# Gate and up projections as 2x2 blocks with seven block products instead of eight

## The reference, cut to what matters

```python
def _swiglu(x, w_in, w_out):
    gate, up = jnp.split(x @ w_in, 2, axis=-1)
    return (jax.nn.silu(gate) * up) @ w_out
...
h = h + 0.5 * _swiglu(_rms_norm(h, g_ffn), w_ffn_in, w_ffn_out)   # D_MODEL = 1024, D_FF = 2816
```

## Time and profile before

| | us |
|---|---|
| median of 3 runs | 2584.19 |
| lowest and highest | 2573.76, 2585.38 |
| the profiled execution | 2584.06 |
| its span, first to last instruction | 2582.3 |

### The profile page before, as it was taken

The page is one execution under the profiler, slowest core; times in us unless marked ns, Lnnn a source line. Parts: engine busy times, 40 slices in busy tenths (PEclk is TensorE's granted clock), DMA queues, the critical chain, the costliest instruction groups (busy, mean ns, idle before and its releaser), DMA issues.

```text
span 2582.3 us, 46166 instructions
## 1 busy us (share of the span) xinstructions
PE 2454.5 (95%) x18130; PEld 2369.9 (92%) x18130; DVE 1158.5 (45%) x1551; ACT 821.8 (32%) x1370; POOL 316.1 (12%) x331
## 2 busy tenths in 40 slices
PE   7999999599898999999999999999979999999997
PEld 7999999588888999999977999999868889999997
DVE  5433443455654544344444443444455545443443
ACT  4222222444544322122322221223245543221221
POOL 2000000243432100000122000001132211000001
PEclk9999999799998999999999999999988889999999
DMA  3232221000000223222223222222211102232221
GB/s 118 89 113 74 89 95 63 28 10 17 11 23 17 90 83 109 73 89 97 68 81 110 89 89 91 82 91 89 82 32 44 34 26 89 88 101 72 89 97 68
DMA packets 84937, 187.18 MB, mean 72 GB/s; under 512 B 42129, under 2 KB 43697, under 8 KB 84865
## 3 DMA queue, kind: packets, MB, share of 16 engines
q1 hardware_dynamic: 83584, 181.68, 22.4%
q0 software_dynamic: 1280, 4.49, 0.5%
HBM read 178.79 MB, written 7.35 MB: 72 GB/s over the span
## 4 chain that ended last, share of the span: by engine, by line
PE 88%; DVE 5%; ACT 3%; issue 2%; POOL 1%; DMA 0%; ACTq 0%; DVEq 0%; POOLq 0%; SPq 0%
PE ps L493 65%; PE ps L468 6%; PE ps L470 6%; PE ps L469 6%; PE ps L712 3%; PE ps L718 1%; PE ps L665 1%; ACT arena L1016 1%; DVE x_lo L1226 1%; POOL stat L1707 1%; DVE stat L1388 0%; DVE stat L1460 0%; DVE rstd L1231 0%; ACT scratch L1051 0%; DVE x_lo L1224 0%
## 5 line engine op out<-in xcount | busy, mean ns | idle before, releaser
L493 PE MATMUL ps<-x_hi,w_hi 128*128 128x272 f32 x2816 | 586.5, 290 | 18.9 <-DVE w_lo L1214 10.1
L493 PE MATMUL ps<-x_hi,w_lo 128*128 128x272 f32 x2816 | 585.0, 289 | 0.0
L493 PE MATMUL ps<-x_lo,w_hi 128*128 128x272 f32 x2816 | 582.8, 289 | 0.0
L1214 DVE TENSOR_TENSOR w_lo<-raw,w_hi 128x1024 fp32r<-128x1024 f32 (+4 forms) x300 | 397.5, 1327 | 301.7 <-ACT w_hi L875 294.0
L493 PEld LDWEIGHTS ps<-x_hi,w_hi 128*128 128x128 f32 x2816 | 445.4, 189 | 21.3 <-issue 10.1
L875 ACT ACTIVATE w_hi<-raw 128x1024 fp32r<-128x1024 f32 (+4 forms) x300 | 328.8, 1099 | 393.6 <-PE ps L493 250.6
L493 PEld LDWEIGHTS ps<-x_lo,w_hi 128*128 128x128 f32 x2816 | 445.0, 190 | 0.0
L493 PEld LDWEIGHTS ps<-x_hi,w_lo 128*128 128x128 f32 x2816 | 441.8, 190 | 0.0
L493 PE MATMUL ps<-hid_hi,w_hi 128*128 128x272 f32 x1664 | 345.5, 289 | 3.6 <-DVE hid_lo L1224 3.6
L493 PE MATMUL ps<-hid_lo,w_hi 128*128 128x272 f32 x1664 | 344.9, 288 | 0.0
L493 PE MATMUL ps<-hid_hi,w_lo 128*128 128x272 f32 x1664 | 344.5, 288 | 0.0
(11 more groups left out here) (207 smaller groups left out, 3230.7 us busy)
## 6 DMA issues: line engine op xcount, KB each, us to landing
raw<-w_ffn_in SPq DMA_DIRECT2D x176, 512.0 KB, 3.5
raw<-w_ffn_out SPq DMA_DIRECT2D x64, 704.0 KB, 4.0
raw<-w_b_kv SPq DMA_DIRECT2D x16, 512.0 KB, 3.6
raw<-w_a_out SPq DMA_DIRECT2D x8, 512.0 KB, 3.6
raw<-w_b_q SPq DMA_DIRECT2D x8, 512.0 KB, 3.6
raw<-w_b_out SPq DMA_DIRECT2D x8, 512.0 KB, 3.6
raw<-w_a_in SPq DMA_DIRECT2D x4, 672.0 KB, 3.9
raw<-w_a_qup SPq DMA_DIRECT2D x8, 288.0 KB, 2.8
```

The lines of the kernel that those rows point to most:

```text
L493: mm = pe.matmul(pair(bank)[:, n, :], w[a], xs[b][:, cols], start=(k == 0 and a + b == 0), stop=(k == kt - 1 and a == 1))
L1214: dve.tensor_tensor(wl[par][:, 0:n], raw[par][:, 0:n], wh[par][:, 0:n].bitcast(F32), ALU.subtract).then_inc(w_lo, 1)
```

## The change

Gate and up weights of one hidden tile are seen as a 2x2 block matrix (rows: gate, up; columns: the first and the last four of the eight model tiles), and x as a 2x2 block matrix too (rows: model tiles 0 to 3 and 4 to 7; columns: token columns 0 to 271 and 272 to 543). Strassen's method in Winograd's form makes the product with seven block products instead of eight: 7 x 4 x 3 = 84 matmuls of 272 columns for a gate/up pair. For it:

- GpSimd makes four sums of weight blocks for each pair (`weight_sums`, four operations of 128x512), two pairs ahead, and also takes over `hid_lo`.
- The weights of a pair come by two loads (up, then gate) into `R`, twelve blocks of 512 columns, of which two sets of four hold the raw weights and four the sums. ScalarE and VectorE split seven blocks per pair in groups "01", "23", "45" (1024 columns each) and "6" (512).
- x is mixed once per stage: VectorE makes four combinations per pair of model tiles (t1 to t4), ScalarE rounds all seven (816 and 1088 columns) and VectorE takes their low parts into `xs`.
- The results are put together from three PSUM banks (two sets of three, by parity) by ScalarE copies p6, p5 and VectorE's u2, u3, up[1], gate[1] and up[0]. Of the norm only gate is multiplied; the factor for up is applied to the result of the "out" part, in two VectorE operations (`e`, `h`) where there was one.
- The constants for MLA and for the second attention are loaded later, since `R` and `xs` share memory with other tiles.

The core of it, the products on TensorE, the sums on GpSimd, one turn on VectorE and on ScalarE:

```diff
@@ tensor, ffn_in @@
+                def times(par, j, k):
+                    w, b = operand(par, j), 3 * par + (2, 0, 1, 2, 0, 1, 2)[j]
+                    w = [a[:, k * P:(k + 1) * P] for a in w]
+                    return product(ps[:, b, 0:HALF_T], w, [xs_part(n, k, j, j + 1) for n in range(2)],
+                                   j in (0, 1, 2, 3) and k == q["order"][0], k == q["order"][DK - 1], j in (4, 5, 6))
...
+                    for j in range(3, 7):
+                        if j == 3:
+                            pe.wait_ge(*st["act"].at("p6", i))
+                        if j == 4:
+                            pe.wait_ge(*ws.at("45", i))
+                            pe.wait_ge(*st["dve"].at("u2", i))
+                        if j == 5:
+                            pe.wait_ge(*st["act"].at("p5", i))
+                        if j == 6:
+                            pe.wait_ge(*ws.at("6", i))
+                            pe.wait_ge(*st["dve"].at("u3", i))
@@ gpsimd @@
+            def weight_sums(q, m, par, free=()):
...
+                pool.wait_ge(*ws["dve"].at("23", i - 1))
+                pool.wait_ge(up_load[par], loads)
+                pool.tensor_tensor(s1, a21, a22, ALU.add).then_inc(inc, 1)
+                pool.wait_ge(*ws["dve"].at("01", i - 1))
+                pool.wait_ge(gate_load[par], loads)
+                pool.wait_ge(*ws["pool"].at("s1", i))
+                pool.tensor_tensor(s2, s1, a11, ALU.subtract).then_inc(inc, 1)
+                pool.tensor_tensor(s3, a11, a21, ALU.subtract).then_inc(inc, 1)
+                pool.wait_ge(*ws["dve"].at("45", i - 1))
+                pool.wait_ge(*ws["pool"].at("s2", i))
+                pool.tensor_tensor(s4, a12, s2, ALU.subtract).then_inc(inc, 1)
...
+                def turn(m, par, more):
+                    if more:
+                        weight_sums(q, m + 1, par)
+                    i = 2 * m + par
+                    pool.wait_ge(*st["act"].at("hid_hi", i))
+                    pool.tensor_tensor(tile(hid[1], i), scratch[3], tile(hid[0], i).bitcast(F32), ALU.subtract
@@ vector, ffn_in, turn(i) @@
+                    dve.tensor_tensor(u2, bx, p6, ALU.add).then_inc(inc, 1)
...
+                        pair_lo(q, i + 1, 1 - par, "01")
+                    dve.wait_ge(*st["pe"].at("m3", i))
+                    dve.wait_ge(*st["dve"].at("u2", i))
+                    dve.tensor_tensor(u3, by, u2, ALU.add).then_inc(inc, 1)
+                    dve.wait_ge(*st["act"].at("p5", i))
+                    dve.wait_ge(*st["pool"].at("hid_lo", i - 1))
+                    dve.wait_ge(*st["dve"].at("u3", i))
...
+                    dve.tensor_tensor(up[1], u3, p5, ALU.add).then_inc(inc, 1)
...
+                        pair_lo(q, i + 1, 1 - par, "23")
+                    dve.wait_ge(*st["pe"].at("m4", i))
+                    dve.tensor_tensor(gate[0], bx, r[0], ALU.mult).then_inc(inc, 1)
+                    dve.wait_ge(*st["pe"].at("m5", i))
+                    dve.tensor_tensor(gate[1], bz, u2, ALU.add).then_inc(inc, 1)
+                    dve.wait_ge(*st["dve"].at("c12", i))
+                    dve.tensor_tensor(gate[1], gate[1], r[1], ALU.mult).then_inc(inc, 1)
+                    if not last:
+                        pair_lo(q, i + 1, 1 - par, "45")
+                    dve.wait_ge(*st["pe"].at("m6", i))
+                    dve.tensor_tensor(up[0], by, u2, ALU.add).then_inc(inc, 1)
...
+                    dve.tensor_tensor(scratch[3], scratch[0], scratch[3], ALU.mult).then_inc(inc, 1)
+                    if not last:
+                        pair_lo(q, i + 1, 1 - par, "6")
@@ scalar, ffn_in, turn(i): p6, "01", p5, "23", "45", silu, "6", hid_hi @@
+                    act.activation(scratch[2][:, 0:HALF_T], ps[:, y, 0:HALF_T], ACT.Copy).then_inc(inc, 1)
...
+                    act.wait_ge(*st["dve"].at("hid", i))
...
+                    act.activation(tile(hid[0], i), scratch[3], ACT.Copy).then_inc(inc, 1)
@@ sync @@
+            def load_pair(q, i, par):
...
+                sp.wait_ge(*q["ws"]["dve"].at("6", i - (1 if isinstance(i, int) and i == 0 else 2)))
+                src, b = d["w_ffn_in"][q["f"], q["half"], i], a_block(par, 0)
+                for n, done in ((2, up_load[par]), (0, gate_load[par])):
+                    sp.dma_start(R[:, b + n:b + n + 2, :].rearrange("p b w -> p (b w)"),
+                                 src[:, n * HB:(n + 2) * HB]).then_inc(done, 16)
```

More of the change, by code:

```diff
@@ L48 @@
 SLOT = FT * P
+DK = KC // 2
+HB = DK * P
+XW = 7 * HALF_T
 NEG = -1.0e30
@@ L292, in ffn @@
                 kind = "honly" if hf == 0 else "last" if gain is None else "update"
-                parts.append(dict(kind="in", u=units(2 * FT, KC * P), st=run("ffn", FT), f=f, half=hf,
-                                  x=None, rms=None))
-                parts.append(dict(kind="out", what=kind, u=units(KC, FT * P), kt=FT, scale=0.5,
-                                  st=run(kind, KC), src=("ffn", f, hf), gain=gain, first=None))
+                q = dict(kind="in", st=run("pair", FT), ws=run("wsplit", FT), f=f, half=hf, n=HALVES * f + hf,
+                         x=None, rms=None, last_unit=unit[0] - 1, order=list(range(DK)), prev=None, second=None, stores=False)
+                if hf == 1:
+                    q["prev"] = parts[-1]
+                    parts[-1]["next"] = q
+                parts.append(q)
+                parts.append(dict(kind="out", what=kind, u=units(KC, FT * P), kt=FT, st=run(kind, KC),
+                                  src=("ffn", f, hf), gain=gain, first=None, before=q, next=None))
+                q["out"] = parts[-1]
             return parts
-        X0 = run("xsplit", KC)
+        X0 = run("xsplit", DK)
         F0 = ffn(0, G_MIX)
@@ L305, in build @@
                  att=run("att", PAIRS))
-        MO = dict(kind="out", what="update", u=units(KC, KC * P), kt=KC, scale=1.0, st=run("update", KC),
-                  src=("a",), gain=G_FFN + 8, first=M)
+        MO = dict(kind="out", what="supdate", u=units(KC, KC * P), kt=KC, st=run("supdate", DK),
+                  src=("a",), gain=G_FFN + 8, first=M, before=None)
         F1 = ffn(1, G_BKV)
+        MO["next"] = F1[0]
         F1[0].update(x=MO["st"], rms=run("rms"))
@@ L318, in build @@
                  att=run("att", PAIRS), fstage=run("fstage", PAIRS))
-        XO = dict(kind="out", what="update", u=units(KC, KC * P), kt=KC, scale=1.0, st=run("update", KC),
-                  src=("b",), gain=G_FFN + 24, first=X)
+        XO = dict(kind="out", what="supdate", u=units(KC, KC * P), kt=KC, st=run("supdate", DK),
+                  src=("b",), gain=G_FFN + 24, first=X, before=None)
         F3 = ffn(3, None)
+        XO["next"] = F3[0]
         F3[0].update(x=XO["st"], rms=run("rms"))
```

581 lines of the change are left out of this document (422 added, 159 removed).

## The result

The changed kernel takes 2612.13 us, the median of four runs (2609.79 to 2613.2), where the kernel before took 2583.82 in the same comparison. The ratio is 1.0108, with a 95% interval of 1.009 to 1.0126: slower by one per cent where it was forecast one per cent faster, and 55 us above the forecast of 2557. It lies outside the forecast's own range (2538 to 2576) and 0.1 us above the top of the wide one (2480 to 2612). The profiled execution took 2609.79 us, its span 2608.0.

What follows compares the result with a forecast made beforehand. VectorE and GpSimd taking turns at SBUF were to bind the gate/up loop at 11.6 us per tile. Terms -53 + 9 + 13 + 0.4 + 3.2 = -27 us gave 2557 us, own range 2538 to 2576, wide range 2480 to 2612.

Steps and rivals of the forecast that it cites:

- the ring: Gate/up loop: VectorE and GpSimd taking turns at SBUF, with their waits, make 11.6 us per tile against TensorE's 10.52.
- the wait ahead of product 3: Gate/up loop: TensorE waits 1.08 us per tile for p6, which stands on ScalarE behind hid_hi.
- hand-over: Shared SBUF access passing between VectorE and GpSimd: overlap leaves 1.09 of 1.23 us and 1.12 of 1.28 to count.
- Rival 1: Gate/up loop: TensorE stays the bound, 10.52 us a tile, total 2479; chance 0.25 with what lies between.
- rival 2: Gate/up loop: no overlap when VectorE and GpSimd swap access, 12.9 us a tile, total 2640; chance 0.24.
- Rival 3: Gate/up loop: second weight load lands 1.6 us later than counted, 0.8 us a tile, total 2615; chance 0.06.
- A half: Gate/up stage half of 11 pairs: 124.7 us after the change, 7.6 less than 132.3; seven halves save 53.
- rival 4: Gate/up loop: TensorE's idling lowers its clock to 1.2 GHz, costing 1.5 us a tile, mostly hidden; no separate chance.
- The start: First half ends at about 161 us instead of 152.3, after serial rounds on x of some 6.5 us: +9.
- MO, XO: Attention out-projections: late second-unit splits, three waits of 1.1 us, and 3.1 at the end: +6.5 each, 13 together.
- Key/value stage: Passage from key/value stage to layer 1: split "23" (1.23) replaces the first low part (0.8): +0.4 us.
- Way out: Result scaled and added in two operations, uncovered only behind the last tile, four times: +3.2 us.

Runs made afterwards that it cites:

- experiment 1: VectorE's four weight-split subtractions read one operand from cleared PSUM banks, against the changed kernel; 2545.83 us, ratio 0.984 to the kernel before.
- Narrow squares: GpSimd's adding of squares at the start, in MO and in XO on 16 of 544 columns, against the changed kernel; 2590.28 us, ratio 1.0017.
- early split: In MO and XO each second weight unit is split ahead of the rounding and low parts of x, against the changed kernel; 2597.99 us, ratio 1.004.
- late reciprocal: In the first pair of F0, F1 and F3 split "23" goes ahead of the reciprocal, against the changed kernel; 2605.2 us, ratio 1.0081.
- narrow sums: GpSimd's weight sums on 16 of 512 columns from the third pair of each half, against the changed kernel; 2522.16 us, ratio 0.9748.
- experiment 4: Ahead of F2 a key/value store is issued behind GpSimd's sums, against the changed kernel: third store 2614.36 us, fourth store 2612.32 us.

## Why the prediction was wrong

**The loops: right.** 10.52 us of TensorE, 11.6 from the ring (11.70), the wait ahead of product 3 behind p6 (0.86 for 1.08), the lengthened instructions and the counting of 1.09 and 1.12 us for a hand-over all stand. Taking VectorE's second SBUF operand out of four subtractions gave 10.58 without any other change in the loop. Rival 1 (10.52) and rival 2 (12.9) are out; the hand-over does overlap, as far as I counted it. Rival 3's 2615 comes near the measured time by chance: late loads cost almost nothing here (below). The sum of the ring is no full model, though: for another order it gave 11.4 to 11.7, and 12.74 was the common pair in seven of eight halves.

The Trainium skill, "SBUF — State Buffer", section "Who interferes with whom", calls the pair of ports that VectorE and GpSimd share an exclusive lock, and says of VectorE's 2-port modes that whoever issues first has it "for the whole instruction". Worked by the letter for this kernel that was the 12.9 of rival 2, and the trace has 11.70. The section also says that a VectorE instruction contends with GpSimd's reads when both its inputs are in SBUF, and not when at most one is. There trace and page agree: 1950 ns with both in SBUF, 1224 with one in PSUM (experiment 1).

**A half: 6.4 us less, not 7.6.** The second halves gained 5.8 to 6.7. F3's, with no irregular pair, takes 125.7 us: eight pairs of about 11.7 and three of 10.6 to 10.9. So my 0.1 us too little for a bound pair, and 0.04 for a free one, make nearly 4 of the 4.8 us that the four halves lack; F0's is 0.9 longer. Loads landed after 4.5 us in the median, where I took 3.5 from the earlier trace rows. GpSimd's second sum waited for one four times, up to 1.4 us; a short and a long pair follow each time instead of two bound ones. Two such couples by the ends of their last products, in F0 and in F1 (same columns as above):

```profile
271.82:282.41 10.59, 10.59 (x87) 10.59 (x86) 9.56 (x12) 5.49 (x8) 8.09 (x6) 1.00 0.29 99
282.41:296.52 14.11, 12.35 (x87) 12.14 (x86) 12.88 (x14) 5.47 (x8) 10.74 (x8) 0.88 0.22 74
...
1143.56:1154.21 10.65, 10.65 (x87) 10.60 (x86) 9.63 (x12) 5.48 (x8) 7.41 (x6) 1.00 0.31 100
1154.21:1166.80 12.59, 10.83 (x87) 10.61 (x86) 12.43 (x14) 5.48 (x8) 9.30 (x6) 1.00 0.26 83
```

In F1 the two take 23.2, nothing lost. In F0 they take 24.7, since TensorE's clock fell there as well, to 0.50 in the window 290 to 292, after it had idled half of 286 to 288. That is rival 3 and rival 4 in small.

**The start, MO, XO: the step that failed.** I worked out one round on x as a chain of operations with nearly their own durations ("some 6.5 us") and put GpSimd "in between" as if it cost tenths. I had just shown that every two-operand instruction of VectorE may wait 1.1 us for GpSimd, and used it only for the loops. A round has six such instructions, and four of them are the shortest of the kernel. Narrow squares show the size: 22 us in the median, 19 of them in the three profiled stages, and a round of 6.35 us without them. The start came to 20.0 for 9, and the last low part of x ended at 45.2 where I had "about 34"; the waits for every second split were 2.3 for 1.1. The early split took most of them away, 14 us in the median. The 2 us for the reciprocal were too small as well: it holds back "23" and with it GpSimd's sums, 6 us over three halves by the late reciprocal (7 in the median).

**First halves of F1 and F3: counted as steady.** I gave them -7.6 each, and 2.5 back in MO's and XO's terms for the last x pair and the reciprocal, but they took 3.0 and 3.4 more than before. In F1's first pair TensorE waits 1.92 us for the last low part of x and 1.76 for u2, and 4.77 ahead of its second pair's product 3:

```profile
931.89 0.59 PE L565 MATMUL ps<-xs_hi,w_hi_more 128*128 128x272 f32 x1 [4.77 <-ACT scratch L1078]
```

That makes 8.45 where I had 2.5. Of the 4.77, 2.66 are left with narrow sums, and 3.40 with the late reciprocal. With narrow sums the half is 12.8 us shorter, 3.4 in its second pair and 9.4 in the nine behind it, which is the ring's part.

**Key/value stage: +4.0 for +0.4.** TensorE idles 6.92 us instead of 4.33. It ended at 1439.5; VectorE's five evictions start at 1441.70, since a low part of x (1439.27, 1.28) and the split "01" (1440.55, 1.23) stand ahead of them, where they started 0.1 us behind TensorE before. I had only priced what follows the evictions. These 2.1 and the longer split make the 2.6; the other 1.4 lie ahead of 1439.5, where TensorE waits as long as before but is busy 1.35 us longer, at a granted clock of 0.96 for 0.97. No run tried them. F2's first half gained 1.9 for 7.6; one sum of GpSimd took 6.64 us at its head (experiment 4), but how much of the missing 5.7 that makes was not tried.

**Way out: right** (+3.5 for +3.2), and the moved constants cost nothing that the trace shows.

The attentions moved by +4.9 and -7.3 with the granted clock and no change in their work; I had put them at 0. The second one took 293.4 to 303.5 us over the kernels here, so a forecast of one execution of this kernel can't be much better than that. The first one took 408.0 before and 410.3 to 413.6 in the fifteen kernels since, so its 4.9 look lasting; what makes them no run shows.

## What to carry to other kernels

Before work goes to GpSimd, list every VectorE instruction with both operands in SBUF that runs beside it, and price each at its own time plus up to one whole GpSimd instruction (here up to 1.1 us, 0.65 to 0.9 in the mean of the loop). Short ones pay the most for their size, so price the stages with a serial chain of them as carefully as the steady loop. An operand in PSUM takes an instruction out of that list at no cost of its own (1224 ns for 1219); copies by ScalarE to get it there gave back 32 of the 66 us that the operand alone was worth, until ScalarE's own order was mended. When one ring is shortened, work out the next longest before moving anything.

## What the runs showed of the hardware

VectorE and GpSimd don't always take turns. In the loops, and between the four short subtractions of the last round at the start, GpSimd got in between two VectorE instructions each time; but when VectorE ran its row of low parts and splits ahead of F2 (1444.99 to 1452.18, seven instructions), GpSimd's sum, issued at 1446.69, got nothing until the row was over, 5.5 us later. It held in three runs (6.64, 6.63 and 7.05 us). What decides between the two behaviours no run here shows.
